# Routing weights through a DRAM table instead of routing matmuls, with U's remainders on VectorE alone

## The chip, the cores and the metric

The kernel runs on one core of one Trainium2 chip. The metric is the device time of one execution in microseconds (us), as the median of the runs. The core's engines are TensorE (PE, its weight loads PEld), VectorE (DVE), ScalarE (ACT), GpSimd (POOL) and SyncE (SP); each works through its own list of instructions in order and waits on semaphores that other engines or transfers raise. 16 DMA engines carry the transfers that SP, ACT and POOL issue.

## The reference, cut to what matters

Two transformer blocks of two layers each are run one after the other on 256 tokens of width 1024, in float32. The change lies in the expert layer (`peer`) that closes both layers of the first block:

```
q = (xb @ w_q).reshape(PEER_BLOCK, PEER_HEADS, PEER_QDIM)       # 8 heads
s1 = einsum('phd,nd->phn', q[..., :half], subkeys[0])           # 128 keys
s2 = einsum('phd,nd->phn', q[..., half:], subkeys[1])           # 128 keys
v1, i1 = top_k(s1, 16);  v2, i2 = top_k(s2, 16)
cand = v1[..., :, None] + v2[..., None, :]                      # 16 x 16 a head
cs, ci = top_k(cand, 16)
e = i1[ci // 16] * 128 + i2[ci % 16]                            # expert numbers
g = softmax(cs)                                                 # 16 weights a head
a = gelu(einsum('pd,phkd->phk', xb, u_tab[e]))
return einsum('phk,phkd->pd', g * a, v_tab[e])
```

Each token picks 8 x 16 = 128 of 16,384 experts (with repeats between heads, whose weights then add up). The rest of both blocks (gated linear attention, windowed attention, mLSTM, latent attention, MLPs) is not touched.

## The kernel before, in words

The kernel does not gather experts. It computes all 16,384 of them for all 256 tokens and multiplies each activation by a routing weight that is zero for the experts that were not chosen. `gate` (128 partitions x 32,768 floats) holds the activations: partition p, column block a, token t is expert 128 a + p. All weights come through one stream of 1 MB slabs into `ring`, which has two slots; SP loads each slab in two halves and waits, before it fills a slot again, until the remainder of the old half has been made (`lo_made`).

Every product of weights is done in pieces to keep float32 accuracy: ScalarE rounds a half slab to `split_hi` (L1562), another engine makes `split_lo` = weights - `split_hi`, and TensorE multiplies both. `split_hi` and `split_lo` have two buffers each, a tile (half slab) apiece, handed over by `hi_made`, `lo_made`, `hi_free` and `lo_free`.

An expert layer runs in these stages:

- **Queries and scores.** Eight slabs of `peer_q`, then 64 score matmuls into `scores`. VectorE makes the remainders and, between them, the products for the modulation strips (L356).
- **U, 64 slabs** (two blocks of 128 experts each). In slabs 0 to 31 (`u_slab`) GpSimd makes the remainders (`split_lo_gpsimd`, L1575), while VectorE makes the whole choice (`peer_choose_vector`): for both token tiles 16 searches for the best 16 of 128 scores, 8 searches among 256 candidates, and the turning of candidate ranks into key numbers. ScalarE takes the exponentials at slab 28, TensorE turns the three lists (row key, column key, weight) by six transposes (`peer_turn_tensor`, L1797), and VectorE stores them in bf16, the weight as three bf16 parts. In slabs 32 to 63 (`paired_tile`) VectorE makes the remainders, adds the two parts of each product (`u_sum_vector`), and ScalarE applies GELU.
- **Routes.** Beside slabs 32 to 63 of U, and again beside slabs 0 to 31 of V, 32 groups of 8 tokens each are done, for one half of the row keys at a time. VectorE compares keys with the tokens' lists and makes one-hot rows and columns (L1831, L1833, L1837), TensorE multiplies them, 24 bf16 matmuls to a group (L1948), and VectorE multiplies the routing weights from PSUM into `gate` (`routes_merge_vector`, L1848).
- **V, 64 slabs.** Each activation block is split as the weights are (`gate_hi` by ScalarE, L1559; `gate_lo` by VectorE, L1585), and TensorE accumulates the output with four matmuls for each of three pairs of parts (L2003). In slabs 32 to 63 VectorE also works through 32 strip products, whose 512 KB each GpSimd loads (L395).

The order within each engine is written out by hand; marks recorded in a first build turn into semaphore values in the second.

Of the kernel before, what the change touches and what calls it, by code (L numbers as in the profile page):

```python
# [34 lines left out]
P = 128  # L35
# [6 lines left out]
RING = 2  # L42
BANK = 512
# [79 lines left out]

TWO_PI = 6.283185307179586
# [5 lines left out]
def build(nc, io, marks):  # L130

    new_marks = {}
    with ExitStack() as ctx:
# [40 lines left out]
        iota = sb("iota", [P, P])  # L174

# [70 lines left out]
        banks_free = sem("routes_banks_free")  # L246
# [15 lines left out]
        hot_rows, hot_cols = sem("hot_rows"), sem("hot_cols")  # L262
        hot_equal = sem("hot_equal")
        mlp_drained, mlp_squared, hid_made = sem("mlp_drained"), sem("mlp_squared"), sem("hid_made")
        routes_full = sem("routes_full")
# [773 lines left out]
        def constants_gpsimd(g):  # L1039
            for buf, val in ((ident, 0.0), (ones, 1.0), (zeros, 0.0), (band, 0.0), (after, 0.0),  # L1040
                             (blockm, 0.0), (upper, 1.0), (gmask_f, 1.0)):
                nc.gpsimd.memset(buf[:, :], val).then_inc(gpsimd_steps, g.step())
            nc.gpsimd.iota(iota[:, :], pattern=[[1, P]], base=0, channel_multiplier=0,
# [366 lines left out]
        peer_qT = gate[:, 80 * SEQ:(80 + 2 * PEER_H) * SEQ].rearrange("p (g n) -> p g n", g=2 * PEER_H)  # L1410
        A = Area(small)
        e_sel = A.take(3, NT, HK)
        top_v = A.take(2 * PEER_H, TOPK)
        top_if = A.take(2 * PEER_H, TOPK)
        top_i = A.take(2 * PEER_H * TOPK).bitcast(U32).rearrange("p (a b) -> p a b", b=TOPK)
        cand = A.take(TOPK * TOPK)
        cand2 = A.take(TOPK * TOPK)
        c_i = A.take(HK).bitcast(U32)
        c_part = A.take(HK).bitcast(U32)
        c_pf = A.take(HK)  # L1420
        match = A.take(4, TOPK, TOPK)
# [3 lines left out]
        HALF = KEYS // 2  # L1425
        GROUP = 8
        W_PARTS = 3

        def take_bf16(*shape):
            n = int(np.prod(shape))  # L1430
            ap = B.take(n // 2).bitcast(BF16)
            return ap.rearrange("p (a b) -> p a b", a=shape[0]) if len(shape) == 2 else ap
        PAIR = 2
        selT = take_bf16(2 + W_PARTS, SEQ * PAIR).rearrange("p n (t q) -> p n t q", q=PAIR)
        keys_bf = take_bf16(1, KEYS)[:, 0, :]
        hot_c = [take_bf16(GROUP, KEYS) for _ in range(2)]
        hot_r = [[take_bf16(GROUP, HALF) for _ in range(W_PARTS)] for _ in range(2)]
        w_left = B.take(SEQ)
# [38 lines left out]
        def peer_score_tensor(t, l):  # L1477
# [37 lines left out]
            with t.eng.Fori(0, 3) as i:  # L1515
                for j in range(8):
                    u_slab(i, j)
            for j in range(6):
                u_slab(3, j)
            peer_turn_tensor(t, l)  # L1520
            for j in range(6, 8):
                u_slab(3, j)
# [16 lines left out]
            def routed(i):  # L1539
                for j in range(8):  # L1540
                    routes_group_tensor(t, i * 8 + (2 * l * GROUPS + j - GROUPS), j % 2)
                    t.eng.wait_ge(u_added, i * 8 + (l * 32 + j - 31))
                    if j == 1:
                        t.eng.wait_ge(u_drained, l * 68 + 36)
                    for e in range(2):
                        paired_tile(i, j, e)
            t.eng.wait_ge(u_drained, l * 68 + 34)
            with t.eng.Fori(4, 8) as i:
                routed(i)
# [14 lines left out]
        def split_lo_gpsimd(g, name, i0, i1):  # L1564


            g.eng.wait_ge(lo_made, i0 * 8 + TILE0[name])
            with g.eng.Fori(i0, i1) as i:
                for j in range(4):
                    slot = (START[name] + j) % RING  # L1570
                    for e in range(2):
                        tile = TILE0[name] + 2 * j + e
                        g.eng.wait_ge(hi_made, i * 8 + (tile + 1))
                        g.eng.wait_ge(lo_free, i * 8 + (tile + 1))
                        nc.gpsimd.tensor_tensor(split_lo[:, e, :], ring[:, slot, e * D:(e + 1) * D],  # L1575
                                                split_hi[:, e, :].bitcast(F32), ALU.subtract).then_inc(lo_made, 1)
            g.seen.clear()
# [12 lines left out]
        def peer_score_scalar(a, l):  # L1590
# [44 lines left out]
            def late_step(i, first):  # L1635
                for j in range(8):
                    for e in range(2):
                        split_hi_scalar(a, f"u{l}", i, j, e, 8)
                    if j == 0 and first:
                        drain(i - 1, 7)  # L1640
                        continue
                    if j >= 2 or not first:
                        late_gelu(i if j >= 2 else i - 1, (j - 2) % 8)
                    late_copy(i if j else i - 1, (j - 1) % 8)

            def step(i, first=False):
                for j in range(8):
                    for e in range(2):
                        if j or not first:
                            split_hi_scalar(a, f"u{l}", i, j, e, 8)  # L1650
                    if j:
                        drain(i, j - 1)
                    elif not first:
                        drain(i - 1, 7)
                    if j == 4 and isinstance(i, int) and i == 3:
                        a.wait_ge(*when(f"chosen{l}"))
                        w = e_sel[:, 2, :, :].rearrange("p a b -> p (a b)")
                        nc.scalar.activation(w, w, ACT.Exp).then_inc(scalar_steps, a.step(f"weights{l}.exp"))
            step(0, True)
            with a.eng.Fori(1, 3) as i:  # L1660
                step(i)
            a.seen.clear()
            step(3)
            late_step(4, True)
            with a.eng.Fori(5, 8) as i:
                late_step(i, False)
# [9 lines left out]
            a.eng.wait_ge(banks_free, (2 * l + 1) * GROUPS + 2)  # L1676
# [20 lines left out]
        def peer_choose_vector(v, l):  # L1697
# [16 lines left out]
            if l == 0:  # L1714
                first_chunks_vector(v, 39, 40)
                trig_vector(v)
            for i in range(NT):
                for g in range(4):
                    v.wait_ge(*when(f"sc{l}.out{i}{g}"))
                for g in range(2 * PEER_H):  # L1720
                    top16(v, scores[:, i, g, :], s_left, top_v[:, g, :], top_i[:, g, :])
                v.wait_ge(vector_steps, v.n)
                nc.vector.tensor_copy(top_if, top_i).then_inc(vector_steps, v.step())
                for h in range(PEER_H):
# [3 lines left out]
                        top_v[:, 2 * h, :].unsqueeze(2).to_broadcast([P, TOPK, TOPK]),  # L1728
                        top_v[:, 2 * h + 1, :].unsqueeze(1).to_broadcast([P, TOPK, TOPK]), ALU.add) \
                        .then_inc(vector_steps, v.step())  # L1730
                    v.wait_ge(vector_steps, v.n)
                    top16(v, cand, cand2, e_sel[:, 2, i, h * TOPK:(h + 1) * TOPK], c_i[:, h * TOPK:(h + 1) * TOPK])
                v.wait_ge(vector_steps, v.n)

                for part, (op, n) in enumerate(((ALU.logical_shift_right, 4), (ALU.bitwise_and, 15))):
                    nc.vector.tensor_scalar(c_part, c_i, n, None, op).then_inc(vector_steps, v.step())
                    v.wait_ge(vector_steps, v.n)
# [1585 lines left out]
```

## Time and profile before

| | |
|---|---|
| device time, median of 3 runs | 2588.92 us (2586.33 to 2589.01) |
| span of the profiled execution, first to last instruction | 2591.7 us |
| TensorE busy | 2514.7 us, 97% |
| VectorE busy | 2119.7 us, 82% |
| ScalarE busy | 1220.0 us, 47% |
| GpSimd busy | 468.9 us, 18% |
| chain that ended last | TensorE 83%, VectorE 7%, GpSimd 3% |
| read from memory, written | 533.42 MB, 3.15 MB |

The profile is one execution; no other time than its span is given for it. The span lies 2.8 us above the median of the runs. A share of busy time is an average over stages, so the stretches of U and V are looked at by themselves below. A line of a group of instructions reads: line of the kernel, engine, operation, written<-read with their shapes, count, then busy time and mean duration in ns, then the idle time in front of them and what ended it.

### The profile page before, as it was taken

To read this page: it belongs to the slowest core of one execution; us is meant where nothing else is said; L and a number is where in the kernel's file an instruction comes from. 1 tells how busy PE (TensorE), PEld (TensorE's weight loads), DVE (VectorE), ACT (ScalarE), POOL (GpSimd) and SP (SyncE) were. 2 spreads that over 40 slices of the span, in tenths; PEclk is the share of its full clock that TensorE was granted. 3 is DMA by queue.
4 is the path that set the end of the run, shared out by engine and by line. 5 is a ranking of instruction groups with operands and counts; after the bars stand their busy time and mean duration, and the time that the engine had idled before them with its cause. 6 is when DMAs were issued, how large, how long until landed. Compare 5 with 4: busy or idle time off the path is not lost.

```text
span 2591.7 us, 48983 instructions
## 1 busy us (share of the span) xinstructions
PE 2514.7 (97%) x17184; PEld 2192.0 (85%) x17184; DVE 2119.7 (82%) x3783; ACT 1220.0 (47%) x1769; POOL 468.9 (18%) x385
## 2 busy tenths in 40 slices
PE   5999999999999999999999999999999999999998
PEld 4789999888888877899998888887878789777987
DVE  7889997888888778869978888887777788777754
ACT  4544444545444545444444554444545554334543
POOL 2115992000000001018980000000101000110000
PEclk8999999999999999999999999999999999999999
DMA  9775555555456887365555445546887567964554
GB/s 345 259 263 168 179 178 172 166 166 185 169 167 211 284 271 272 130 220 171 183 179 166 162 166 185 170 168 231 282 286 256 189 222 262 318 242 163 171 183 149
DMA packets 147831, 538.38 MB, mean 208 GB/s; under 512 B 16609, under 2 KB 16865, under 8 KB 147442
## 3 DMA queue, kind: packets, MB, share of 16 engines
q1 hardware_dynamic: 114226, 414.78, 46.9%
q0 software_dynamic: 32752, 119.24, 13.2%
q10 hardware_dynamic: 720, 2.62, 0.3%
q8 instruction: 79, 1.29, 0.2%
q14 instruction: 54, 0.44, 0.1%
HBM read 533.42 MB, written 3.15 MB: 207 GB/s over the span
## 4 chain that ended last, share of the span: by engine, by line
PE 83%; DVE 7%; POOL 3%; issue 3%; DMA 2%; ACT 2%; SPq 0%; DVEq 0%; POOLq 0%; ACTq 0%
PE ps L2003 26%; PE ps L1529 9%; PE ps L2748 7%; PE ps L748 6%; PE ps L1505 6%; PE ps L1457 5%; PE ps L1533 5%; PE ps L2730 5%; PE ps L1948 3%; PE ps L1509 3%; POOL split_lo L1575 3%; PE ps L2734 2%; DVE gate L928 1%; DMA gate<-in_mod 1%; PE ps L2142 1%
## 5 line engine op out<-in xcount | busy, mean ns | idle before, releaser
L1562 ACT ACTIVATE split_hi<-ring 128x1024 fp32r<-128x1024 f32 x760 | 801.0, 1056 | 757.8 <-PE ps L1509 199.8
L1587 DVE TENSOR_TENSOR split_lo<-ring,split_hi 128x1024 fp32r<-128x1024 f32 x572 | 698.5, 1222 | 177.0 <-ACT split_hi L1562 172.2
L1575 POOL TENSOR_TENSOR split_lo<-ring,split_hi 128x1024 fp32r<-128x1024 f32 x128 | 339.9, 2672 | 91.2 <-ACT split_hi L1562 90.9
L1559 ACT ACTIVATE gate_hi<-gate 128x256 fp32r (+1 forms) x252 | 105.4, 418 | 405.4 <-PE ps L2003 398.9
L2003 PE MATMUL ps<-split_hi,gate_hi 128*128 128x512 f32 x1024 | 285.1, 398 | 1.5 <-DVE gate_lo L1585 1.5
L2003 PE MATMUL ps<-split_hi,gate_lo 128*128 128x512 f32 x1024 | 278.2, 392 | 5.1 <-DVE gate_lo L1585 5.0
L2003 PE MATMUL ps<-split_lo,gate_hi 128*128 128x512 f32 x1024 | 278.0, 391 | 0.0
L1505 PE MATMUL ps<-h_parts,split_hi 128*128 128x256 f32 x2048 | 266.9, 283 | 0.0
L1529 PE MATMUL ps<-h_parts,split_hi 128*128 128x512 f32 x1024 | 261.6, 397 | 0.0
L1505 PEld LDWEIGHTS ps<-h_parts,split_hi 128*128 128x128 f32 x2048 | 254.9, 192 | 0.0
L2003 PEld LDWEIGHTS ps<-split_hi,gate_lo 128*128 128x128 f32 x1024 | 192.6, 189 | 48.4 <-DVE gate_lo L1585 7.5
L2003 PEld LDWEIGHTS ps<-split_lo,gate_hi 128*128 128x128 f32 x1024 | 191.8, 188 | 43.6 <-DVE split_lo L1587 3.3
L2003 PEld LDWEIGHTS ps<-split_hi,gate_hi 128*128 128x128 f32 x1024 | 187.7, 189 | 40.6 <-ACT split_hi L1562 2.8
L1529 PEld LDWEIGHTS ps<-h_parts,split_hi 128*128 128x128 f32 x1024 | 183.5, 189 | 32.7
L1585 DVE TENSOR_TENSOR gate_lo<-gate,gate_hi 128x256 fp32r<-128x256 f32 x252 | 106.8, 424 | 113.7 <-ACT split_hi L1562 112.2
L395 POOL DMA_DIRECT2D mod_w<-in_mod x64 | 33.8, 528 | 694.7 <-DVE strip_part L356 688.8
L1533 PEld LDWEIGHTS ps<-h_parts,split_lo 128*128 128x128 f32 x1024 | 139.7, 190 | 10.2
L1509 PE MATMUL ps<-h_parts,split_lo 128*128 128x256 f32 x1024 | 145.1, 284 | 2.0 <-POOL split_lo L1575 2.0
L436 POOL DMA_DIRECT2D small<-in_mod x104 | 55.1, 530 | 490.5 <-DVE modc L356 459.9
L1533 PE MATMUL ps<-h_parts,split_lo 128*128 128x256 f32 x1024 | 142.5, 282 | 0.0
L1837 DVE TENSOR_TENSOR small<-small 128x512 bf16<-128x512 bf16 x384 | 139.7, 421 | 0.0
L356 DVE CUSTOM_DVE_ANT_0 small<-small,gate,cols 128x1024 f32<-128x1024 f32 x104 | 131.9, 1280 | 6.1 <-DMA small<-in_mod 6.1
(405 smaller groups left out, 3951.0 us busy)
## 6 DMA issues: line engine op xcount, KB each, us to landing
ring<-in_stream SPq DMA_DIRECT2D x776, 512.0 KB, 4.3
small<-in_mod POOLq DMA_DIRECT2D x104, 512.0 KB, 5.6
mod_w<-in_mod POOLq DMA_DIRECT2D x64, 512.0 KB, 5.2
gate<-in_mod POOLq DMA_DIRECT2D x44, 512.0 KB, 6.9
gate<-in_mod SPq DMA_DIRECT2D x8, 512.0 KB, 16.2
gate<-in_mod ACTq DMA_DIRECT2D x4, 512.0 KB, 8.3
x_kept<-x POOLq DMA_DIRECT2D x8, 256.0 KB, 3.9
gate<-x_kept POOLq DMA_DIRECT2D x4, 512.0 KB, 8.5
```

The costliest lines, as they stand in the source:

```text
L356: return nc.vector.tensor_tensor_reduce(out=w, in0=w, in1=c_act, scale=1.0, scalar=start, op0=ALU.mult, op1=ALU.add, accum_out=out)
L748: return nc.tensor.matmul(ps[:, banks[2 * nb + i], :], src[:, b * per + n, i * P:(i + 1) * P], w[:, b % 2, at_:at_ + BANK], start=(b == n ...
L1505: nc.tensor.matmul(out, split_hi[:, e, c * P:(c + 1) * P], part[:, c, :], start=(part is hT_hi and c == 0), stop=False)
L1509: ins = nc.tensor.matmul(out, split_lo[:, e, c * P:(c + 1) * P], hT_hi[:, c, :], start=False, stop=(c == DC - 1))
L1529: nc.tensor.matmul(ps[:, bank, :].rearrange("p (a n) -> p a n", a=2), split_hi[:, e, c * P:(c + 1) * P], h_parts[:, :, c, :], start=(c == ...
L1533: ins = nc.tensor.matmul(ps[:, bank, SEQ:2 * SEQ], split_lo[:, e, c * P:(c + 1) * P], hT_hi[:, c, :], start=False, stop=(c == DC - 1), ski ...
L1562: nc.scalar.activation(split_hi[:, e, :], ring[:, slot, e * D:(e + 1) * D], ACT.Copy).then_inc(hi_made, 1)
L1575: nc.gpsimd.tensor_tensor(split_lo[:, e, :], ring[:, slot, e * D:(e + 1) * D], split_hi[:, e, :].bitcast(F32), ALU.subtract).then_inc(lo_m ...
L1587: nc.vector.tensor_tensor(split_lo[:, e, :], ring[:, (START[name] + j) % RING, e * D:(e + 1) * D], split_hi[:, e, :].bitcast(F32), ALU.sub ...
L1837: ins = nc.vector.tensor_tensor(pairs(hot_r[r][m]), equal, of_token(2 + m, HALF), ALU.mult)
L2003: return nc.tensor.matmul(ps[:, 2 * nb + n, :], g[:, e, n * P:(n + 1) * P], w[:, e, nb * BANK:(nb + 1) * BANK], start=opens, stop=True, sk ...
L2748: return nc.tensor.matmul(ps[:, 4 + 2 * nb + n, :], h[:, c0, n * P:(n + 1) * P], w[:, e, nb * BANK:(nb + 1) * BANK], start=(first and h is ...
```

## The change

The routing weights no longer pass through TensorE. Two tables in DRAM, one for each layer, hold a float32 weight for each expert and token (128 x 128 x 256). They are cleared by transfers, filled by indirect transfers that add, and read back a piece for each V slab.

- **Clearing.** SP writes each table in 16 pieces of 1 MB from a zeroed buffer: layer 0's between the slab loads of `gla_v`, `gla_og`, `gla_out` and `peer_q0`, layer 1's between the loads of the first slabs of `u0`.
- **Choice.** It is made in four batches of two heads for both token tiles. VectorE makes U's remainders itself from slab 0 on (`POOL_SLABS = 0`) and puts pieces of the choice between them; `UTiles` counts the priced microseconds of choice against an allowance of 1.4 us a tile up to tile 64 and 1.0 after. The match of ranks with keys is done twice a batch, in three pieces priced 1.5, 1.25 and 1.25 us. ScalarE takes each batch's exponentials at slabs 9, 21, 32 and 48.
- **Scatter.** For each batch, head, token tile and rank GpSimd issues one indirect transfer of 128 weights (one for each token of the tile) to 128 places of the table, 256 in each layer. Before a head's 16 it waits for those of the head before, same token tile, to have landed.
- **V.** When all have landed, GpSimd loads the first four pieces (256 KB each); later ones are issued by ScalarE. VectorE multiplies each into `gate` in one instruction, a slab ahead. The 32 strip products now spread over all 64 slabs of V.

The routing matmuls, the transposes, the one-hot instructions and their semaphores go. The core of the diff:

```
+POOL_SLABS, HEAD_START = 0, 1.4
+EXP_AT = [9, 21, 32, 48]
+CLEARS = 16
...
+        BATCHES, PER = 4, 2
+        route_in = [B.take(2, SEQ) for _ in range(ROUTE_RING)]
...
-            def routed(i):
+            def paired(i):
                 for j in range(8):
-                    routes_group_tensor(t, i * 8 + (2 * l * GROUPS + j - GROUPS), j % 2)
                     t.eng.wait_ge(u_added, i * 8 + (l * 32 + j - 31))
...
+        def routes_gpsimd(g, l):
+            g.eng.wait_ge(routes_cleared[l], 16 * CLEARS)
+            routes = io["routes"][l].rearrange("a p t -> (a p t)").unsqueeze(1)
+            for b in range(BATCHES):
+                g.wait_ge(*when(f"weights{l}.{b}"))
+                for hh in range(PER):
+                    for i in range(NT):
+                        head = (l * BATCHES + b) * PER + hh
+                        g.wait_ge(routes_added[i], 16 * TOPK * head)
+                        for k in range(TOPK):
+                            n = (i * PER + hh) * TOPK + k
+                            g.eng.indirect_dma_start(
+                                out=routes,
+                                out_offset=bass.IndirectOffsetOnAxis(ap=r_index[:, b, n:n + 1].bitcast(U32), axis=0),
+                                in_=r_weight[:, b, n:n + 1], in_offset=None, compute_op=ALU.add) \
+                                .then_inc(routes_added[i], 16)
+            for i in range(NT):
+                g.wait_ge(routes_added[i], 16 * HK * (l + 1))
+            for slab in range(ROUTE_RING):
+                g.eng.dma_start(route_in[slab], routes_of(l, slab)).then_inc(first_routes_landed, 16)
...
+            for b in range(BATCHES):
+                choose_batch_vector(v, l, b, paced)
+            paced.through(EXP_AT[BATCHES - 1] + 1)
+            weights_vector(v, l, BATCHES - 1)
+            paced.through(64)
...
+            def after(self, us):
+                self.spent += us
+                while self.spent > 0:
+                    share = HEAD_START if self.tile == 2 * POOL_SLABS else 1.4 if self.tile < 64 else 1.0
+                    if self.tile == 2 * POOL_SLABS and self.spent < share:
+                        return
+                    self.one()
+                    self.spent -= share
...
+                for hh in range(PER):
+                    for q in range(2):
+                        top16(v, scores[:, i, 2 * (PER * b + hh) + q, :], s_left, top_v[:, at_(i, hh, q), :],
+                              top_i[:, at_(i, hh, q), :])
+                        paced.after(1.57)
+                        n_top += 1
+                        if b and n_top == 3:
+                            weights_vector(v, l, b - 1)
...
+                    top16(v, cand, cand2, w[:, n:n + TOPK], c_i[:, n:n + TOPK])
+                    paced.after(2.83)
...
+            routes_merge_vector(v, l, 0)
+            first_slab_vector(v, l)
+            routes_merge_vector(v, l, 1)
+            for slab in range(1, 64):
+                if slab < 63:
+                    routes_merge_vector(v, l, slab + 1)
                 for e in range(2):
+                    split_lo_vector(v, f"v{l}", slab // 8, slab % 8, e)
+                if slab in (2, 3):
+                    strip_part_vector(v, l, slab - 2)
+                elif slab > 4 and slab % 2:
+                    strip_part_vector(v, l, (slab - 1) // 2)
...
+            for slab in range(1, 64):
+                a.wait_ge(routes_merged, 64 * l + slab + 1)
+                if slab + ROUTE_RING < 64:
+                    route_load_scalar(a, l, slab + ROUTE_RING)
...
+                    if a in FIRST_CLEARS:
+                        clear_routes(0, 4 * FIRST_CLEARS.index(a) + s - a)
+                    if a == START["peer_q0"]:
+                        for q in range(2):
+                            clear_routes(0, 12 + 2 * (s - a) + q)
...
+                    if a == START["u0"]:
+                        with sp.Fori(1, 1 + CLEARS) as i:
+                            pair(i)
+                            clear_routes(1, i - 1)
...
-                split_lo_gpsimd(g, f"u{l}", 0, 8)
+                split_lo_gpsimd(g, f"u{l}", POOL_SLABS)
+                routes_gpsimd(g, l)
                 strip_loads_gpsimd(pool, l)
```

## Rows read from the trace of the kernel before

**Rows 1.** Busy time of all engines by stretch; then granted clock, DMA share, GB/s

```profile
220.00:408.00 188.00, 187.00 (x1548) 185.67 (x1547) 167.91 (x447) 88.06 (x103) 168.75 (x64) 1.00 0.54 178
814.00:995.00 181.00, 178.40 (x772) 143.92 (x772) 140.00 (x203) 86.43 (x126) 16.88 (x32) 1.00 0.82 279
```

**Rows 2.** TensorE in order of time (start, length), middle of layer 0's U

```profile
405.33 2.08 PE L1505 MATMUL ps<-h_parts,split_hi 128*128 128x256 f32 x16
...
408.21 0.87 PE L1948 MATMUL ps<-small 128*128 128x64 bf16 x24
408.92 2.08 PE L1529 MATMUL ps<-h_parts,split_hi 128*128 128x512 f32 x8
...
414.59 0.87 PE L1948 MATMUL ps<-small 128*128 128x64 bf16 x24
```

**Rows 3.** TensorE in order of time, start of layer 0's V

```profile
619.32 0.87 PE L1948 MATMUL ps<-small 128*128 128x64 bf16 x24 [0.24 <-DVE small L1837]
...
622.88 1.07 PE L2003 MATMUL ps<-split_hi,gate_hi 128*128 128x512 f32 x4
...
625.60 0.87 PE L1948 MATMUL ps<-small 128*128 128x64 bf16 x24
```

**Rows 4.** The routing matmuls' line: count, ns min/median/max, first and last

```profile
L1948 PE MATMUL ps<-small x3072: 193/193/204, 408.2 to 1755.5; 128*128 128x64 bf16 x192
```

**Rows 5.** TensorE in order of time, the transposes of layer 1

```profile
1343.41 0.81 PE L1797 MATMUL ps<-ident,small 128*128 128x128 f32 x6
1343.98 2.16 PE L1505 MATMUL ps<-h_parts,split_hi 128*128 128x256 f32 x16
```

**Rows 6.** VectorE in order of time, query stage and first searches of U

```profile
196.65 1.22 DVE L1587 TENSOR_TENSOR split_lo<-ring,split_hi 128x1024 fp32r<-128x1024 f32 x1 [0.45 <-ACT split_hi L1562]
197.79 1.28 DVE L356 CUSTOM_DVE_ANT_0 gate<-gate,cols 128x1024 f32<-128x1024 f32 x1
...
199.53 1.23 DVE L1587 TENSOR_TENSOR split_lo<-ring,split_hi 128x1024 fp32r<-128x1024 f32 x1 [0.45 <-ACT split_hi L1562]
...
217.91 0.29 DVE L1688 MAX8 small<-gate 128x8 f32<-128x128 f32 x1 [0.68 <-ACT gate L1616]
...
219.50 0.28 DVE L1688 MAX8 small<-gate 128x8 f32<-128x128 f32 x1
```

**Rows 7.** Groups of VectorE's instructions, 612 to 1000 us

```profile
L1585 DVE TENSOR_TENSOR gate_lo<-gate,gate_hi 128x256 fp32r<-128x256 f32 x126 | 53.4, 424 | 56.3 <-ACT split_hi L1562 55.8
...
L1848 DVE TENSOR_TENSOR gate<-gate,ps 128x512 f32 x24 | 16.3, 681 | 0.0
```

**Rows 8.** Groups of VectorE's instructions, 200 to 420 us

```profile
L1749 DVE TENSOR_TENSOR small<-small 128x1024 f32<-128x1024 f32 x8 | 26.6, 3325 | 0.3
...
L1753 DVE TENSOR_REDUCE small<-small 128x64 f32<-128x1024 f32 x8 | 9.8, 1220 | 0.3
```

**Rows 9.** Groups of GpSimd's instructions, whole span

```profile
L369 POOL DMA_DIRECT2D gate<-in_mod x40 | 21.1, 529 | 133.7 <-DVE modc L356 133.7
```

**Rows 10.** Transfers: count, KB each, median us from issue to landing

```profile
x_kept<-x POOLq DMA_DIRECT2D x8, 256.0 KB, 3.9
...
c_loop<-c_kept POOLq DMA_DIRECT2D x2, 512.0 KB, 5.3
```

**Rows 11.** TensorE's busy time by stretch; then granted clock, DMA share, GB/s

```profile
1036.00:1040.00 4.00, 4.00 (x19) 1.00 1.02 413
...
1056.00:1060.00 4.00, 1.71 (x12) 0.94 0.00 0
1060.00:1064.00 4.00, 4.00 (x21) 0.50 0.00 0
1064.00:1068.00 4.00, 4.00 (x20) 0.50 0.00 0
```

**Rows 12.** All engines by stretch, GLA stage; then clock, DMA share, GB/s

```profile
100.00:120.00 20.00, 18.50 (x88) 14.46 (x87) 13.98 (x25) 9.90 (x12) 2.64 (x5) 1.00 0.78 310
...
140.00:160.00 20.00, 19.47 (x102) 16.24 (x101) 19.23 (x32) 7.98 (x14) 5.49 (x10) 1.00 0.97 355
```

More of the change, by code:

```diff
@@ L1513, in u_slab @@
                     ins.then_inc(lo_free, 1)
-            with t.eng.Fori(0, 3) as i:
+            with t.eng.Fori(0, 4) as i:
                 for j in range(8):
                     u_slab(i, j)
[L1518 to L1522, printed above, removed]
             def paired_tile(i, j, e):
@@ L1562, in split_hi_scalar, with split_lo_gpsimd @@
             nc.scalar.activation(split_hi[:, e, :], ring[:, slot, e * D:(e + 1) * D], ACT.Copy).then_inc(hi_made, 1)
[L1564 to L1577, printed above, removed]
+        def split_lo_gpsimd(g, name, slabs):
+            for j in range(slabs):
+                for e in range(2):
+                    tile = TILE0[name] + 2 * j + e
+                    g.wait_ge(lo_made, tile)
+                    g.wait_ge(hi_made, tile + 1)
+                    g.wait_ge(lo_free, tile + 1)
+                    nc.gpsimd.tensor_tensor(split_lo[:, e, :], ring[:, (START[name] + j) % RING, e * D:(e + 1) * D],
+                                            split_hi[:, e, :].bitcast(F32), ALU.subtract).then_inc(lo_made, 1)
@@ L1633, in late_gelu, with weights_exp @@
                                      u_part[:, :, :].rearrange("p a n -> p (a n)"), ACT.Gelu).then_inc(u_drained, 1)
-            def late_step(i, first):
-                for j in range(8):
+            def weights_exp(b):
+                a.wait_ge(*when(f"chosen{l}.{b}"))
+                nc.scalar.activation(r_weight[:, b, :], r_weight[:, b, :], ACT.Exp) \
+                    .then_inc(scalar_steps, a.step(f"weights{l}.exp{b}"))
+            for s in range(64):
+                i, j = s // 8, s % 8
+                if s:
                     for e in range(2):
                         split_hi_scalar(a, f"u{l}", i, j, e, 8)
[L1639 to L1666, printed above, removed]
+                if s in EXP_AT:
+                    weights_exp(EXP_AT.index(s))
+                if 0 < s <= 32:
+                    drain((s - 1) // 8, (s - 1) % 8)
+                if s == 33 and l == 0:
+                    a.eng.wait_ge(routes_cleared[1], 16 * CLEARS)
+                if s >= 34:
+                    late_gelu((s - 2) // 8, (s - 2) % 8)
+                if s >= 33:
+                    late_copy((s - 1) // 8, (s - 1) % 8)
             late_gelu(7, 6)
@@ L1716, in peer_choose_vector @@
                 trig_vector(v)
-            for i in range(NT):
[L1718 to L1724, printed above, removed]
+            v.wait_ge(lo_made, TILE0[f"u{l}"])
@@ L2049, in peer_out_scalar @@
                     table_ahead_scalar(a, ACT.Sqrt)
-            for first, last in ((1, 4), (4, 8)):
-                a.eng.wait_ge(banks_free, (2 * l + 1 + first // 4) * GROUPS + 2)
-                with a.eng.Fori(first, last) as i:
-                    for j in range(8):
-                        for e in range(2):
-                            split_hi_scalar(a, f"v{l}", i, j, e, 8)
             a.seen.clear()
@@ L3119, in _, with pair @@
                 if end - a > 4:
-                    with sp.Fori(1, (end - a) // RING) as i:
+                    def pair(i):
                         for j in range(RING):
@@ L3317 @@
         io["c_kept"] = nc.dram_tensor("c_kept", (2, D), F32, kind="Internal").ap()
+        io["routes"] = [nc.dram_tensor(f"routes{l}", (KEYS, KEYS, SEQ), F32, kind="Internal").ap() for l in range(2)]
         io["x_kept"] = nc.dram_tensor("x_kept", (P, NT, D), F32, kind="Internal").ap()
```

339 lines of the change are left out of this document (145 added, 194 removed).

## The prediction

> **What bounds the kernel now.** I read the page first: TensorE is busy for 97% of the span and holds 83% of the chain that ended last. Then the busy times by stretch, to see whether that is so where the change works. In the first half of layer 0's U stage TensorE is busy for 187 of 188 us, and in the second half of its V stage for 178.4 of 181 us, at a granted clock of 1.00 both times [rows 1]. So a saving on TensorE counts at full length there, and a saving on another engine counts nothing. Next TensorE's instructions in order of time give the price of each piece. A tile in U's first half starts every 2.88 us (405.33 to 408.21, where the next work begins), so a slab takes 5.76 us. A group of 24 routing matmuls holds the queue for 0.71 us (408.21 to 408.92), and the slab behind it takes 5.67 us (408.92 to 414.59) [rows 2]. A V tile takes 2.72 us (622.88 to 625.60), so a slab takes 5.44 us [rows 3].
>
> **What goes.** 3072 routing matmuls were issued, 24 to a group, so 128 groups [rows 4]. 128 x 0.71 = 90.9 us, all on the path. The six transposes of the chosen lists cost 0.57 us (1343.41 to 1343.98) [rows 5], once in each layer: 1.1 us. The wait of 0.24 us for a routing operand at V's start [rows 3] is there in each layer: 0.5 us. Together 92.5 us, 46.25 us to a layer. Nothing else on TensorE changes, so U's floor becomes 32 x 5.76 + 32 x 5.67 = 184.3 + 181.4 = 365.7 us from its first matmul.
>
> **VectorE takes all of U's remainders.** One takes 1.22 us. The change allows 1.4 us of the choice for each tile in the first half: 2.62 of 2.88 us. The query stage already runs like that: a remainder and a 1.28 us strip product alternate, and the remainders start 2.88 us apart, the rate of TensorE's tiles (196.65 to 199.53) [rows 6]. In the second half a slab asks for 2 x 1.22 + 0.68 for adding the two parts (the nearest row, of the same 128x512 shape [rows 7]) + 2 x 1.0 of choice = 5.12 of 5.67 us. I cost this at nothing. The cover is two remainder buffers, which ride out one piece of 2.83 us; should VectorE fall behind, TensorE waits tile by tile. In V a slab asks for 2 x (0.42 + 1.22) + 0.68 for the merge [rows 7], and 1.28 more on every second slab: 3.96 and 5.24 of 5.44 us, also hidden.
>
> **When the scatters can start.** By the diff's prices a batch of the choice costs 8 x 1.57 + 4 x 2.83 + 2 x (1.5 + 1.25 + 1.25) + 0.6 = 32.5 us of VectorE. The trace bears out the first: one search to the next is 1.59 us (217.91 to 219.50) [rows 6]. The products of the match took 3.33 us on the mean beside GpSimd's remainders, while a one-input reduction over the same 128x1024 took 1.22 us [rows 8]; with GpSimd's remainders gone I take the short time. Batch 0's weights are divided after three more searches, at (32.5 + 4.7) / 2.8 = 13.3 slabs, 76.6 us into U. The four batches are 130.0 us of choice: 32 x 2.8 = 89.6 by the middle, the other 40.4 at 2.0 a slab, so batch 3 is ready at slab 32 + 20.2, 184.3 + 114.5 = 298.8 us into U. That leaves 66.9 us for its 64 transfers, and 289.1 us for all 256 of a layer.
>
> **The price of one indirect transfer** is the number that decides, and no row shows it. Below stands the 0.53 us for which GpSimd issues a plain transfer of 128 partitions [rows 9]: a list of addresses will not be cheaper than none. Above, I let each also wait out one VectorE remainder of 1.22 us: 1.75 us. I take 1.1, about the middle, since neither row is nearer. It covers issue and drain together: 32 thousand element-sized additions in each layer's table may also be slower to drain than to issue.
>
> The Trainium skill ("SBUF — State Buffer", section "Who interferes with whom") says that a VectorE instruction with two SBUF inputs contends with a GpSimd instruction that reads SBUF, and that one of them then blocks fully. The 3.33 against 1.22 us [rows 8] agree. An indirect transfer reads its list from SBUF, so the rule speaks for the upper end, while plain transfers only write descriptors; no row shows which side an indirect one falls on.
>
> **The end of U.** After the last issue comes its landing (3.9 us, as x_kept's write), four issues of 0.53, the landing of the first four pieces of the table (5.3 us, as c_loop's load [rows 10]) and, before TensorE's first V matmul, the merge, 0.68, and a gate copy of about 0.4 us: 12.4 us. VectorE's merge stands ahead of the last U sum and of V's remainders; ScalarE's wait for it stands ahead of its gate copies; GpSimd's strip loads stand behind the scatters. All of them wait together, with V's first slabs already loaded. With x us for a transfer the delay is the larger of 64x - 66.9 and 256x - 289.1, plus 12.4: at 1.1 it is 3.5 + 12.4 = 15.9 us. An idle TensorE also lost its clock: after 4 us with 1.71 us of matmuls the granted clock was 0.50 (1.2 of 2.4 GHz) in the next two windows [rows 11], and 9 us at half speed lose 4.5 us. So 20.4 us to a layer, 40.8 in all.
>
> The Trainium skill ("DMA: Bandwidth & Descriptors", section "Anatomy of one DMA — SWDGE (gpsimd) path") puts the fixed part of a GpSimd transfer at about 2.0 us. By it the last landing is an estimated 1.9 us shorter, and the total 3.8 us lower.
>
> **The clears.** Two tables of 128 x 128 x 256 x 4 bytes, 16.8 MB each, are written from SP's queue, 1 MB at a time between the slab loads. The engines move at most about 413 GB/s [rows 11]. Layer 0's falls into the GLA stage, where they already moved 310 GB/s at 100 to 120 us and 355 at 140 to 160, with shares of 0.78 and 0.97 [rows 12]. At worst none of it is hidden: 16.8 MB / 413 GB/s = 41 us. At best, nothing: the slabs are asked for two ahead. Eight slabs of 1 MB with 8 MB of clears and, at the 0.5 MB a slab of V's second half, 4 MB of strips make 20 MiB, 21.0 MB; at 413 GB/s that is 51 us, against 44 us for eight slabs at V's 5.44; the ring and the pauses between the products absorb part, and x_kept's write, which ScalarE waits for, shares the engines. I take 6 us. Layer 1's table is cleared in U's first half of layer 0: 1.5 MB a slab in 5.76 us. V's second half carried 1.5 MB a slab with 2.6 us of TensorE idle [rows 1]; I take 2 us, between 0 and 41 again. V now carries 1 + 0.25 of table + 0.25 of strips, the same 1.5 MB, as its second half did: 0, and up to 2.6 us in each of four halves. A table piece is asked for three slabs, 16 us, before its merge.
>
> **Sum.** 2591.7 - 92.5 + 8 + 40.8 = 2548.0 us. The profiled span is 2.8 us above the median of the runs, 2588.92; kept as it is, that gives 2545 us.
>
> **Rivals.**
> - *Scatters hidden.* At x up to 0.8 us, 64 x 0.8 - 66.9 + 12.4 is below zero and V starts on time: 2588.9 - 92.5 + 8 = 2504 us. For it: the 0.53 us of a plain issue; against it: the list to be read and the additions in memory. Chance 0.17.
> - *GpSimd becomes the bound of U* (the slower side). From x = 1.23 us on, 256 transfers overrun U by more than is won: 256 x 1.23 - 289.1 + 12.4 + 4.5 = 42.7 us, plus 4 of clears, against 46.25. Place: V's first merge. At 1.5 us the delay is 94.9 + 12.4 + 4.5 = 111.8 us to a layer, and the time 2588.9 - 92.5 + 8 + 223.6 = 2728 us; at 1.75, 2856. For it: VectorE is busy nearly all through U, and GpSimd and VectorE did lengthen each other [rows 8]; against it: a plain issue is short of it by a factor of 2. Chance 0.29.
> - *The clears are not hidden.* 41 us instead of 6 in the GLA stage: 2580 us. For it the 0.97 share [rows 12], against it the pauses between the products. Chance 0.08.
> - *The forecast*, x from 0.8 to 1.23, 2504 to 2589 us: chance 0.46.
>
> **Chances.** A difference under 0.2% (5 us) is about what a measurement of this kernel can't tell from none; that is the strip of x from 1.22 to 1.24, which I give 0.05 of the forecast's share. Faster: 0.17 + 0.08 + 0.41 = 0.66. Slower: 0.29. The range goes from 2500 (scatters hidden, half of the clears too) to 2680, which is x = 1.41 us; I leave 0.13 above it and 0.04 below. The forecast's own range is 2504 to 2589.
>
> **What would show it.** Right: no routing matmuls; U tiles still 2.88 us apart with VectorE's remainders; GpSimd starting one indirect transfer about every 1.1 us, batch 0 some 77 us and batch 3 some 299 us after U's first matmul; an idle TensorE of about 16 us before V, and a granted clock below 1.00 right after it; V slabs of 5.44 us. Wrong: transfers more than 1.23 us apart, or a drain that lags the issue (GpSimd waiting on its own earlier transfers); TensorE waiting for split_lo within U; GLA's products waiting for slabs.

## The result and the profile after

The changed kernel takes 2981.69 us (median of 4 runs, 2978.72 to 2982.69) against 2588.97 us for the kernel before (4 runs, 2586.33 to 2591.22): a ratio of 1.152, 95% interval [1.150, 1.153]. The time lies above the range of the prediction. The profiled execution spans 2980.1 us.

The page's first part: busy time, share of the span and instructions of each engine; then the chain that ended last, by engine.

```profile
PE 2412.6 (81%) x14100; PEld 2111.3 (71%) x14100; DVE 1940.2 (65%) x3321; ACT 1235.2 (41%) x1787; POOL 1024.4 (34%) x779
...
PE 71%; issue 18%; DVE 6%; DMA 3%; ACT 2%; SPq 0%; POOL 0%; DVEq 0%; ACTq 0%
```

TensorE has lost the 3072 routing matmuls and 102 us of busy time, and still the kernel takes 393 us longer (2981.69 - 2588.97): TensorE now stands idle. The waits of all engines say where (engine, line, operand <- who released it: us in total, times, longest):

```profile
DVE gate L1858 <- DMA small<-routes: 492.1, 2, 246.9
...
PEld ps L1966 <- issue: 490.6, 8, 245.4
PE ps L1966 <- issue: 488.8, 2, 245.3
```

Read from below: TensorE waits twice, once in each layer, for its first V matmul (L1966). VectorE's first merge (L1858) waits as long, for the first pieces read back from the table. Busy time by stretch answers [rows 1]: U's two halves and the gap behind it (columns as there).

```profile
220.00:404.00 184.00, 184.00 (x1540) 184.00 (x1539) 160.74 (x418) 93.13 (x113) 86.47 (x47) 1.00 0.85 257
404.00:595.00 191.00, 187.68 (x1095) 165.58 (x1093) 140.03 (x238) 111.23 (x137) 164.44 (x85) 1.00 0.78 193
595.00:840.00 245.00, 3.05 (x7) 2.48 (x8) 4.47 (x7) 2.67 (x5) 197.65 (x132) 0.50 0.24 7
```

TensorE is full to U's end; then for 245 us only GpSimd (POOL, 197.65) works. What it does, and at what price, stands in the indirect transfers' own line of the source: count, duration in ns (min/median/max), first and last start; under it, what GpSimd's idle time before them waited for.

```profile
L1583 POOL DMA_INDIRECT routes<-small x512: 1538/1542/2587, 303.5 to 1962.8; - x171
its engine sat idle before it (us, times) until:
  issue: 156.7, 508
  DVE small L1699: 107.9, 1
  DVE small L1700: 104.8, 1
  DVE small L1697: 0.6, 2
```

512 transfers, none shorter than 1.54 us, with 156.7 / 508 = 0.31 us between two of them in which GpSimd waited for nothing that the profile shows. VectorE's choice held it up ahead of the first transfer of each layer (107.9 and 104.8 us) and hardly again; for a transfer of its own it never waited. TensorE's instructions in order of time (start, length) around the gap answer [rows 3]:

```profile
227.92 2.16 PE L1507 MATMUL ps<-h_parts,split_hi 128*128 128x256 f32 x16
...
527.27 2.00 PE L1526 MATMUL ps<-h_parts,split_hi 128*128 128x512 f32 x8
...
530.06 2.00 PE L1526 MATMUL ps<-h_parts,split_hi 128*128 128x512 f32 x8
...
590.56 1.11 PE L1530 MATMUL ps<-h_parts,split_lo 128*128 128x256 f32 x8
836.95 1.19 PE L1966 MATMUL ps<-split_hi,gate_hi 128*128 128x512 f32 x2 [245.28 <-issue]
...
842.86 0.62 PE L1966 MATMUL ps<-split_hi,gate_lo 128*128 128x512 f32 x2
```

U starts at 227.92 (220.47 before) and ends 245.28 us ahead of 836.95, at 591.67. Two matmuls take 1.05 to 1.19 us for the first 5 us of V and 0.62 from 842.86 on.

### The profile page after: what moved, and what is told of

The parts are those of the page before. It is cut to its first block, busy times and chain, and to the rows that moved or that the text cites. A ratio compares the mean times of both kernels' runs of the same rounds, so it can differ in the third digit from the quotient of the medians.

```text
span 2980.1 us, 40708 instructions
## 1 busy us (share of the span) xinstructions
PE 2412.6 (81%) x14100; PEld 2111.3 (71%) x14100; DVE 1940.2 (65%) x3321; ACT 1235.2 (41%) x1787; POOL 1024.4 (34%) x779
## 4 chain that ended last, share of the span: by engine, by line
PE 71%; issue 18%; DVE 6%; DMA 3%; ACT 2%; SPq 0%; POOL 0%; DVEq 0%; ACTq 0%
PE ps L1966 23%; PE ps L1507 8%; PE ps L1526 8%; PE ps L2707 6%; PE ps L756 5%; PE ps L1459 4%; PE ps L1511 4%; PE ps L1530 4%; PE ps L2689 4%; PE ps L2693 2%; DMA ring<-in_stream 1%; ACT split_hi L1558 1%; DVE gate L936 1%; DMA gate<-in_mod 1%; DVE split_lo L1607 1%
## 5 line engine op out<-in xcount | busy, mean ns | idle before, releaser
L1583 POOL DMA_INDIRECT routes<-small x512 | 888.6, 1736 | 370.1 <-issue 156.7
L1607 DVE TENSOR_TENSOR split_lo<-ring,split_hi 128x1024 fp32r<-128x1024 f32 x700 | 853.0, 1220 | 243.0 <-ACT split_hi L1558 238.3
L1966 PE MATMUL ps<-split_hi,gate_hi 128*128 128x512 f32 x1024 | 279.9, 393 | 490.6 <-issue 488.8
L1966 PEld LDWEIGHTS ps<-split_hi,gate_hi 128*128 128x128 f32 x1024 | 193.3, 189 | 533.8 <-issue 490.6
L1858 DVE TENSOR_TENSOR gate<-gate,small 128x512 f32<-128x512 f32 x128 | 87.5, 685 | 492.1 <-DMA small<-routes 492.1
L1966 PE MATMUL ps<-split_lo,gate_hi 128*128 128x512 f32 x1024 | 278.0, 392 | 0.0
L1966 PE MATMUL ps<-split_hi,gate_lo 128*128 128x512 f32 x1024 | 277.9, 391 | 0.0
L1555 ACT ACTIVATE gate_hi<-gate 128x256 fp32r<-128x256 f32 x252 | 105.8, 420 | 347.2 <-PE ps L1966 347.2
L1966 PEld LDWEIGHTS ps<-split_hi,gate_lo 128*128 128x128 f32 x1024 | 193.2, 189 | 41.6 <-DVE gate_lo L1605 1.2
L1966 PEld LDWEIGHTS ps<-split_lo,gate_hi 128*128 128x128 f32 x1024 | 193.0, 189 | 41.9 <-DVE split_lo L1607 1.8
L1688 ACT ACTIVATE gate_hi<-gate 128x256 fp32r<-128x256 f32 x4 | 1.4, 408 | 491.2 <-DVE gate L1858 491.2
```

The costliest lines, as they stand in the source:

```text
L1583: g.eng.indirect_dma_start(out=routes, out_offset=bass.IndirectOffsetOnAxis(ap=r_index[:, b, n:n + 1].bitcast(U32), axis=0), in_=r_weight[ ...
L1607: nc.vector.tensor_tensor(split_lo[:, e, :], ring[:, (START[name] + j) % RING, e * D:(e + 1) * D], split_hi[:, e, :].bitcast(F32), ALU.sub ...
L1966: return nc.tensor.matmul(ps[:, 2 * nb + n, :], g[:, e, n * P:(n + 1) * P], w[:, e, nb * BANK:(nb + 1) * BANK], start=opens, stop=True, sk ...
```

## What an indirect transfer costs

The four stretches of layer 0's 256 transfers, this line's instructions alone (length, GpSimd busy and count, granted clock, DMA share, GB/s):

```profile
303.00:404.00 101.00, 86.47 (x47) 1.00 0.96 272
404.00:525.00 121.00, 103.47 (x58) 1.00 0.80 201
525.00:591.00 66.00, 57.81 (x24) 1.00 0.77 190
592.00:827.00 235.00, 196.31 (x128) 0.51 0.23 0
```

Half of the transfers run after U, when VectorE does nothing: 235 / 128 = 1.84 us apart, with the DMA engines busy for 0.23 of the time. Beside U they are 2.15, 2.09 and 2.75 us apart. Over the layer the spacing is (827.1 - 303.5) / 256 = 2.045 us. The slowest stretch in order of time, VectorE and GpSimd:

```profile
547.34 1.22 DVE L1607 TENSOR_TENSOR split_lo<-ring,split_hi 128x1024 fp32r<-128x1024 f32 x1 [1.57 <-ACT split_hi L1558]
547.49 2.49 POOL L1583 DMA_INDIRECT routes<-small  x1 [0.30 <-issue]
548.55 0.69 DVE L1866 TENSOR_TENSOR u_part<-u_part,ps 128x512 f32<-128x512 f32 x1
550.13 1.23 DVE L1607 TENSOR_TENSOR split_lo<-ring,split_hi 128x1024 fp32r<-128x1024 f32 x1 [0.90 <-ACT split_hi L1558]
551.25 1.54 POOL L1583 DMA_INDIRECT routes<-small  x1 [1.27 <-issue]
```

The transfer that begins 0.15 us into the remainder of 547.34, with 1.07 us of it left, lasts 2.49 us, 0.95 longer. The one of 551.25 lasts 1.54, but the pause ahead of it is 1.27 instead of 0.30 us and falls beside the remainder of 550.13: there the same 0.97 us is lost ahead of the transfer. The remainder keeps its 1.22 us. Since 2.49 + 0.30 = 2.79 us is also the distance of two tiles (527.27 to 530.06 above), nearly every transfer meets the next remainder at the same point, and GpSimd runs in step with TensorE's tiles. The theory after this reading: the gap is GpSimd's time to issue 256 transfers, 1.54 + 0.30 us each, plus what VectorE's two-input remainders add. The rival: the additions in memory drain too slowly, and the instruction only shows it.

The Trainium skill ("SBUF — State Buffer", section "Who interferes with whom") says that a `tensor_tensor` with both inputs in SBUF, which these remainders are, contends with what GpSimd reads there, and that a `tensor_reduce` on this chip never contends; experiment e3 below agrees, with 1.54 us beside reductions of 1.22 us in the same place.

## The experiments

All are edits of the changed kernel, except the last. "Wait" is TensorE's before layer 0's V, 245.3 us in the changed kernel; a spacing x follows from it by (wait + 288.2 - 9.8) / 256, where 288.2 us run from the first transfer to U's end (303.5 to 591.7) and 9.8 from the last issue's end to the first V matmul (827.1 to 836.95).

**Without the adding (e1_plain).** The table is overwritten, so experts that two heads chose get one weight instead of the sum.

```
- in_=r_weight[:, b, n:n + 1], in_offset=None, compute_op=ALU.add)
+ in_=r_weight[:, b, n:n + 1], in_offset=None)
```

> The changed kernel with plain scatters instead of adding ones: the sums over an expert that two heads of a token share are left out. Issue theory (GpSimd needs 1.54 us and a gap of 0.30 us to issue an indirect transfer, whatever the memory does with it): TensorE still waits about 245 us before each V, time 2960 to 2990 us, GpSimd's instruction still 1.54 us at least. Drain rival (adding four bytes at a time into DRAM holds the transfers back): issues come closer together, near the 0.53 us of a plain issue to 1.1 us, and the time falls to 2490 to 2545 us.

2677.57 us, ratio 1.034 [1.030, 1.038]: between the two. The line of the transfers:

```profile
L1583 POOL DMA_INDIRECT routes<-small x512: 954/959/2008, 307.9 to 1664.5; - x171
```

The instruction itself is shorter, 0.96 instead of 1.54 us, and GpSimd still waits for no transfer of its own. So adding costs 0.58 us a transfer. By this run alone it could be a drain that holds the instruction back; e5 and e4 below speak against that, and the price counts as GpSimd's issue. The wait is 94.7 us, x = 1.46. The issue theory holds; its assumption that adding is free to issue does not. VectorE and GpSimd in order of time:

```profile
551.66 1.23 DVE L1607 TENSOR_TENSOR split_lo<-ring,split_hi 128x1024 fp32r<-128x1024 f32 x1 [1.57 <-ACT split_hi L1558]
...
552.49 1.23 POOL L1583 DMA_INDIRECT routes<-small  x1 [0.30 <-issue]
```

This transfer begins with 0.40 us of the remainder left and lasts 0.27 longer than 0.96. With the 0.95 for 1.07 us above, the loss is the rest of the remainder less 0.12 to 0.13 us, as if the transfer waited for its end.

**A one-input operation in place of U's remainder (e3_one_input).** The low parts of U's weights are not computed; a sum over the ring's slab of the same length stands in their place.

```
- nc.vector.tensor_tensor(split_lo[:, e, :], ring[...], split_hi[:, e, :], ALU.subtract)
+ nc.vector.tensor_reduce(split_lo[:, e, 0:64], ring[...] as (a b), b=16, AX, ALU.add)   # u0, u1 only
```

> The changed kernel with U's weight remainders replaced by a VectorE reduction of the same 1.22 us that reads one operand from SBUF instead of two: U's low parts are left out. Issue theory: the floor of 1.84 us a transfer stays and only the lengthening beside VectorE's remainders (2.79 us apart in the last 66 us of U) goes: 256 x 1.845 - 288 + 10 = 194 us of wait before each V instead of 245, time about 2880 us. Port rival (waiting behind VectorE makes most of the price): transfers about 1.1 us apart, time under 2600 us. If VectorE does not matter at all: 2982 us.

2888.57 us, ratio 1.116 [1.112, 1.120], as the issue theory expected; wait 197.7 us, x = 1.86. VectorE and GpSimd in order of time, in the stretch shown above for the changed kernel:

```profile
546.54 1.22 DVE L1609 TENSOR_REDUCE split_lo<-ring 128x64 fp32r<-128x1024 f32 x1 [0.90 <-ACT split_hi L1558]
547.39 1.54 POOL L1583 DMA_INDIRECT routes<-small  x1 [0.30 <-issue]
549.23 1.54 POOL L1583 DMA_INDIRECT routes<-small  x1 [0.30 <-issue]
549.34 1.22 DVE L1609 TENSOR_REDUCE split_lo<-ring 128x64 fp32r<-128x1024 f32 x1 [1.57 <-ACT split_hi L1558]
...
578.48 0.69 DVE L1872 TENSOR_TENSOR u_part<-u_part,ps 128x512 f32<-128x512 f32 x1
578.75 1.54 POOL L1583 DMA_INDIRECT routes<-small  x1 [0.30 <-issue]
```

The transfers of 547.39 and of 549.23 run beside an operation as long as the remainder and stay at 1.54 us. The edit also writes less (64 columns instead of 1024), but what is written is not the cause: the sum of 578.48 writes 512 columns, has one input in SBUF and the other in PSUM, and the transfer that begins inside it stays at 1.54 as well. So the second input from SBUF is what lengthened them; it cost 245.3 - 197.7 = 47.6 us a layer, and 1.84 us of each transfer have nothing to do with it.

**Both together (e8_plain_one_input).** The two edits above at once.

> Indirect transfers without the adding, as e1_plain, and U's weight remainders made by a one-input operation of the same length, as e3_one_input (both change what is computed). If the two savings add up (the adding 0.58 us in GpSimd's instruction, the contention with VectorE's two-input remainders the rest), a transfer costs 0.96 + 0.30 = 1.26 us all through U, the wait ahead of V is 256 x 1.26 - 288 + 12 = 46 us per layer and the time 2575 to 2605. If the contention was only with the adding, e1_plain had none left and the time stays at 2660 to 2690.

2605.44 us, ratio 1.0057 [1.0039, 1.0075], at the upper edge of the first theory. The transfers' line and TensorE's longest wait:

```profile
L1583 POOL DMA_INDIRECT routes<-small x512: 955/962/2016, 308.1 to 1591.2; - x171
```

```profile
PE ps L1972 <- issue: 113.7, 2, 57.0
```

57 us in a layer, x = 1.31: not quite the floor of 1.26, since some transfers still last up to 2.0 us. The trace shows what lengthens these: 12 of layer 0's 256 last over 1.02 us, and 11 of them begin inside an operation of the choice with two inputs in SBUF (the other is the layer's first). One that begins 0.05 us into a product of the match, with 1.18 us left, lasts 2.01. Two pauses of 3.7 and 1.7 us in front of transfers stay unexplained. The waits form a table, and neither saving takes the place of the other:

| wait ahead of layer 0's V, us (x) | two-input remainder | one-input operation |
|---|---|---|
| adding | 245.3 (2.05) | 197.7 (1.86) |
| no adding | 94.7 (1.46) | 56.8 (1.31) |

**Half the indices (e5_64).** Each transfer carries 64 of its 128 weights; the others are not routed.

```
- ap=r_index[:, b, n:n + 1] ...      in_=r_weight[:, b, n:n + 1] ...
+ ap=r_index[0:64, b, n:n + 1] ...   in_=r_weight[0:64, b, n:n + 1] ...
```

> The changed kernel with 64 instead of 128 indices in each transfer, as many transfers as before: the routing weights of half of the tokens are left out. Fixed price: still 1.84 us apart at least, time 2940 to 2982 us. Price by the index (rival): about half, 0.9 to 1.0 us apart, which U hides but for its last batch, time 2490 to 2530 us. A price of two halves (about 1.2 us fixed and 0.6 by the indices): some 1.5 us apart, time about 2750 us.

2886.88 us, ratio 1.115 [1.111, 1.119], wait 196.4 us:

```profile
L1583 POOL DMA_INDIRECT routes<-small x512: 1392/1409/2466, 305.5 to 1870.0; - x171
```

1.41 instead of 1.54 us: 64 indices and additions fewer save 0.13 us. If the other 64 would save as much, an estimated 0.26 of the 1.84 us goes with the indices and 1.58 with the transfer as such. A slow drain would have been halved with the data; with the DMA engines at 0.23 in the gap, it isn't what sets the price. It lies under the range of the fixed-price theory because the mean falls by 1736 - 1549 = 187 ns: the shorter transfers also lose less to the remainders.

**Fewer transfers (e2_half, e2_quarter).** Only ranks 0 to 7, or 0 to 3, of each head's 16 experts are routed; everything else is as in the changed kernel.

```
- for k in range(TOPK):        # and TOPK, HK in the two counts waited for
+ for k in range(8):           # 4 in e2_quarter
```

> The changed kernel with half of the transfers, ranks 0 to 7 of each head; the other half of the routing weights is left out. By the issue theory the first three batches keep up, and the last one's 32 transfers, issued beside VectorE's remainders at 2.75 us, take 88 of 67 us: a wait of about 21 + 12 us before each V and a time of 2545 to 2570 us. If the price were 1.84 us there too, no wait but the 12 us and about 2510 us. If the loss did not follow from the number of transfers (rival: table loads and merges in V, or the clears): well above 2600 us.

> The changed kernel with a quarter of the transfers, ranks 0 to 3 of each head; the rest of the routing weights is left out. Everything else of the change is there: clears, paced choice, table loads, merges. Issue theory: 16 transfers in the last batch at 2.75 us end before U does, no wait before V, and the change shows its gain from the removed matmuls less the clears: 2480 to 2510 us. Rival (another part of the change costs time that the wait covers now): 2520 us or more.

2534.64 us, ratio 0.979 [0.977, 0.982], and 2487.13 us, ratio 0.961 [0.958, 0.964]. With a half, the last batch's 32 transfers (527.6 to 605.0) pass U's end and TensorE waits 22.4 us; it is a little faster than expected, since the 32 take 79 us and not 88. With a quarter nothing is late. TensorE in order of time at U's end, e2_quarter:

```profile
592.27 1.11 PE L1530 MATMUL ps<-h_parts,split_lo 128*128 128x256 f32 x8
593.22 0.63 PE L1966 MATMUL ps<-split_hi,gate_hi 128*128 128x512 f32 x2
```

and its busy time by stretch, U and then V:

```profile
228.00:596.00 368.00, 367.99 (x2588) 345.30 (x2588) 299.24 (x633) 202.87 (x244) 129.38 (x69) 1.00 0.78 233
596.00:950.00 354.00, 352.55 (x1562) 290.16 (x1561) 277.54 (x398) 178.60 (x263) 20.93 (x40) 1.00 0.84 286
```

So layer 1's clears, table reads, VectorE's remainders and the merge are all hidden in U and V, and only layer 0's clears, ahead of U, cost some 7 to 12 us (see the clears below); the loss of the changed kernel is the number of transfers times their price.

**Plain transfers (e4_direct, e7_direct_spread).** GpSimd sends the same 128 x 4 bytes to fixed places, with no list and no adding: side by side in e4, 1 KB apart in e7, as the table's rows are. The table then holds the weights in the wrong places.

```
- g.eng.indirect_dma_start(out=routes, out_offset=..., in_=r_weight[:, b, n:n + 1], compute_op=ALU.add)
+ g.eng.dma_start(routes[at_:at_ + P], r_weight[:, b, n:n + 1])                            # e4
+ g.eng.dma_start(<column at_ of the table's first 128 rows>, r_weight[:, b, n:n + 1])     # e7
```

> The changed kernel with each indirect transfer replaced by a plain GpSimd transfer of the same 128 four-byte weights to fixed addresses of the table: the scatter by index and the sums are left out. Issue theory (it is the indexing that GpSimd pays for): 0.5 to 0.7 us an issue, all hidden in U, at most some 12 us of wait before each V, time 2485 to 2515 us. Rival (128 four-byte pieces are slow to issue or to drain however they are addressed): about 2980 us.

> As e4_direct (GpSimd sends each group's 128 weights of four bytes by a plain transfer to fixed places, no index list, no adding), but the 128 places of one transfer lie 1 KB apart, as the real table's do, where e4's lay side by side. Theory A (the write rate of e4 was low because neighbouring four-byte writes fell on the same place of the memory): GpSimd's waits for its own transfers, 121.9 us in e4, fall below 30 us, the weight stream isn't starved (ScalarE's wait for its slabs under U near zero, 398.4 us in e4) and the time is near e2_quarter's, 2487 to 2530. Rival B (the rate of issue alone, 0.54 us a transfer in place of 1.26 or 1.85, fills the DMA engines with four-byte packets): as e4, 2690 to 2770, DMA share 1.00 while they run.

e4 took 2731.14 us, ratio 1.055 [1.043, 1.067], far from expected: issue is indeed 0.54 us, without the pause of 0.30 (the first 32 take 16.96 us in a row), but the writes drain late and the weight stream with them. The transfers' line, and waits of e4 (columns as above):

```profile
L1584 POOL DMA_DIRECT2D routes<-small x512: 537/538/555, 305.0 to 1700.1; - x171
```

```profile
ACT split_hi L1558 <- DMA ring<-in_stream: 398.4, 96, 21.2
...
POOL routes L1584 <- DMA routes<-small: 121.9, 14, 19.5
```

and of e7:

```profile
ACT split_hi L1558 <- DMA ring<-in_stream: 202.2, 73, 9.3
...
POOL routes L1584 <- DMA routes<-small: 28.0, 12, 6.9
```

A drain that lags shows in GpSimd's waits (121.9 us) and not in its instruction, which stays within 0.537 and 0.555 us; in the changed kernel it was the other way round. Busy time from 300 to 360 us, in which both send some 60 transfers, first e4:

```profile
300.00:360.00 60.00, 38.02 (x281) 37.41 (x279) 27.47 (x82) 13.01 (x15) 29.80 (x57) 0.80 1.00 131
```

then e7:

```profile
300.00:360.00 60.00, 50.62 (x382) 50.21 (x381) 40.37 (x111) 20.33 (x24) 34.02 (x64) 0.89 0.93 211
```

and the changed kernel, which sends 27 there:

```profile
300.00:360.00 60.00, 60.00 (x503) 60.00 (x502) 52.05 (x120) 29.46 (x35) 48.56 (x27) 1.00 0.96 277
```

e7 took 2567.51 us, ratio 0.991 [0.989, 0.993]: between its theories, so each seems to have a part. Spreading the writes is worth 2731 - 2568 = 164 us and frees GpSimd (28.0 us of waits), but the weight stream still comes late; e7 is 2567.5 - 2487.1 = 80 us above e2_quarter. The share of busy DMA engines does not tell the three apart (1.00, 0.93 and 0.96); what they moved does (131, 211 and 277 GB/s). At 1.26 us apart or more (e1) as many four-byte writes did no such harm: ScalarE waited 35.7 us for the stream there, 30.2 in the changed kernel. Why neighbouring writes cost more was not tested and stays open.

**The kernel before with two weight parts (e6_two_parts).** It keeps the routing matmuls, 16 instead of 24 to a group, and leaves out the third bf16 part of each weight.

```
- W_PARTS = 3
+ W_PARTS = 2
```

> The kernel before, with the routing weight in two bf16 parts instead of three: 16 matmuls to a routing group instead of 24, on the same path; the third part's bits of the weight are left out. If the groups stand on the path as the prediction had it, a group takes 0.24 us less, 128 groups 30 us: about 2558 us. If VectorE or the hand-over bounds these stretches (rival): 2585 us or more.

2563.27 us, ratio 0.990 [0.987, 0.992], 1% under the kernel before. A group now holds TensorE for 0.47 us:

```profile
487.78 0.64 PE L1948 MATMUL ps<-small 128*128 128x64 bf16 x16
488.25 2.08 PE L1529 MATMUL ps<-h_parts,split_hi 128*128 128x512 f32 x8
```

128 x (0.71 - 0.47) = 30.7 us, against 31.1 between the two profiled spans (2591.7 and 2560.6) and 25.4 between the medians (2588.70 for the kernel before in the same runs); the interval of the ratio covers 20 to 34 us. The routing matmuls are cheapened where they stand, with no new resource asked for.

## Why the prediction was wrong

**The step that failed** is the price of one indirect transfer: "I take 1.1, about the middle", between 0.53 and 1.75 us. It is 2.045. The bounds were built on the wrong floor. The upper one took a plain issue of 0.53 us and added one whole remainder; the contention was not what was missed (0.95 us where a remainder is met, against the 1.22 allowed), but the transfer alone, with its pause, is 1.84 us, above that bound. The runs split it: 0.54 for a plain issue (e4), 0.42 more for the indirect form (e1: 0.96), 0.58 for adding, a pause of 0.30 that plain transfers don't have, and on the mean 0.2 for the remainders. The pause was no term of the sum at all. "32 thousand element-sized additions in each layer's table may also be slower to drain than to issue" was not the cause here (e5); a slow drain, of plain writes, was seen only when the issue was made much faster (e4).

**The formula around it held.** 256 x 2.045 - 289.1 + 12.4 = 246.8 us; 245.3 and 243.5 were measured. The rival that came true is "GpSimd becomes the bound of U", which decides from 1.23 us on; its place, V's first merge, was named right. e8 came near that edge: at x = 1.31 the kernel is 0.6% slower than before, where the forecast's terms give 2588.9 - 92.5 + 8 + 2 x (256 x 1.31 - 289.1 + 12.4 + 4.5) = 2631 us. With x = 2.045 they give 2588.9 - 92.5 + 8 + 2 x 251.3 = 3007 us, 25 above the measured 2981.69; the smaller terms below make up some 21 of that, and 4 stay open.

- *What goes*: undersized. A slab with a group took 6.38 us before (a group at 503.91, the next at 510.29); without one it takes 2 x 2.79 = 5.59, so a group cost 0.79 and not 0.71: the first product behind a group was longer too (2.08 and 2.00 us). In V a slab went from 6.28 (from one group to the next, [rows 3]) to 5.44 (1008.17 to 1013.61). Some 64 x 0.08 + 64 x 0.13 = 13 us more than the 90.9.
- *VectorE takes all of U's remainders*: right. U takes 591.67 - 227.92 = 363.8 us, forecast 365.7, and TensorE waits for nothing in it. The products of the match fell to 1.22 us, as taken from [rows 8].
- *When the scatters can start*: right. The first is issued 303.52 - 227.92 = 75.6 us into U, forecast 76.6; in e2_half, where U begins at 230.66, the last batch's first is at 527.61, 297.0 us in, forecast 298.8.
- *The end of U*: 9.8 us from the last issue to the first matmul, forecast 12.4: the last transfer has landed 2.0 us after its issue ended, not 3.9, and the first pieces land in 3.2 us, not 5.3, while their four issues take 3.0 instead of 2.1. The half clock after the gap was there (granted 0.50, the 1.2 GHz level, from 836 to 842 us), but ended after 6 us and cost 3 us to a layer, not 4.5.
- *The clears*: somewhat undersized in the GLA stage, 227.92 - 220.47 = 7.5 us, forecast 6; in the profiles of the eight edits of the changed kernel U begins 9.2 to 12.1 us later than before. In two stretches of that stage the DMA engines are busy throughout, against [rows 12], and TensorE for less:

```profile
100.00:120.00 20.00, 16.23 (x68) 12.32 (x69) 9.72 (x12) 7.59 (x10) 2.64 (x5) 0.91 1.03 416
...
160.00:180.00 20.00, 17.15 (x116) 15.02 (x115) 14.69 (x35) 10.37 (x21) 2.38 (x5) 0.91 1.04 412
```

  Layer 1's clears, forecast 2 us, cost nothing: TensorE is busy for 184.00 of 184 us beside them.

The argument also had a choice that should have gone the other way: with a floor that no row showed, and 512 repeats, the middle between two unrelated rows was no reason to hold 1.1 likelier than 1.5.

## What to carry to other kernels

Work that leaves a full engine pays only if its new engine fits: count the new instructions, and put price and count against the stretch that is to hide them (here 289.1 us / 256 = 1.13 us) before looking at anything else. An operation that the trace doesn't show has its floor above its nearest simpler relative's, so the bound above must be widened by each thing that it does more, and by the pause to the next one. If a price per transfer and not per element decides, make fewer and larger transfers, or cheapen the work where it stands.

## What the runs showed of the hardware

- An indirect transfer of 128 four-byte elements holds GpSimd for 0.96 us, with adding 1.54 us, and the next follows 0.30 us later; with 64 elements it is 1.41 us.
- Started inside a VectorE operation with two inputs in SBUF it lasts longer by the rest of that operation less 0.12 to 0.13 us (0.95 longer with 1.07 left, 0.27 with 0.40 left), and can fall into step with it; beside a one-input operation of the same 1.22 us it keeps its 1.54 us.
- Transfers of 128 four-byte writes, issued every 0.54 us, slow the other streams: 131 GB/s at a DMA share of 1.00 with the writes side by side, 211 GB/s at 0.93 with 1 KB between them, against 277 GB/s at 0.96 with indirect transfers 2.15 us apart.
